# Softmax attention: results copied out of PSUM by ScalarE, the split a step later, one gate projection beside the first softmax

## The reference

```python
# first block, layer 2: 16 heads of 64, 4 kv heads, window 128, context keys, a sink
m = max(max(s_lat), max(s_ctx), sink); p = exp(s - m)
den = sum(p_lat) + sum(p_ctx) + exp(sink - m)
o = (p_lat @ v_lat + p_ctx @ v_ctx) / den;  y = o @ w_out
# second block, each layer: 8 heads of 64, 2 kv heads
q = rope(rms_norm(h @ w_q)); k = rope(rms_norm(h @ w_k)); v = h @ w_v
y_attn = softmax(q k^T / 8) v * silu(h @ w_g)
out = (sigmoid(ga) * (y_attn @ w_br_attn) + sigmoid(gg) * (y_gla @ w_br_gla)
       + sigmoid(gs) * (y_sgu @ w_br_sgu)) @ w_out
```

## Time and profile before

| | |
|---|---|
| median of 3 runs | 3404.61 us (3398.12 to 3415.74) |
| the profiled execution | 3406.66 us, of it a span of 3404.9 us |
| TensorE busy | 3108.3 us (91%) |
| VectorE busy | 1914.2 us (56%) |
| ScalarE busy | 1180.5 us (35%) |
| GpSimd busy | 210.3 us (6%) |
| DMA | 323.92 MB, mean 95 GB/s |
| chain that ended last | TensorE 75%, VectorE 11%, ScalarE 8%, issue 4% |

### The profile page before, as it was taken

The page is one execution under the profiler, slowest core; times in us unless marked ns, Lnnn a source line. Parts: engine busy times, 40 slices in busy tenths (PEclk is TensorE's granted clock), DMA queues, the critical chain, the costliest instruction groups (busy, mean ns, idle before and its releaser), DMA issues.

```text
span 3404.9 us, 43105 instructions
## 1 busy us (share of the span) xinstructions
PE 3108.3 (91%) x17878; PEld 2574.3 (76%) x17878; DVE 1914.2 (56%) x2796; ACT 1180.5 (35%) x1795; POOL 210.3 (6%) x138
## 2 busy tenths in 40 slices
PE   7997889999999788999989899988999998998898
PEld 6877778888886666777877788865788776776677
DVE  7856646656434574777644543457354645455655
ACT  4225342212223454322243333325222543433432
POOL 0003100000010000000000320000000202200000
PEclk9999899999998899999989999999999999999999
DMA  5554123333321002555432222310213222230123
GB/s 209 168 169 137 44 68 125 126 126 126 100 69 60 16 1 64 166 175 175 145 82 70 73 77 73 99 32 1 96 51 129 89 72 84 87 115 26 63 96 124
DMA packets 100091, 323.92 MB, mean 95 GB/s; under 512 B 14310, under 2 KB 20326, under 8 KB 98744
## 3 DMA queue, kind: packets, MB, share of 16 engines
q1 hardware_dynamic: 89812, 291.29, 26.5%
q10 hardware_dynamic: 10084, 29.87, 2.5%
HBM read 301.46 MB, written 19.66 MB: 94 GB/s over the span
## 4 chain that ended last, share of the span: by engine, by line
PE 75%; DVE 11%; ACT 8%; issue 4%; DMA 1%; POOL 1%; ACTq 0%; SPq 0%; DVEq 0%; POOLq 0%
PE PS L388 74%; ACT whi L198 2%; ACT Pq L1289 1%; PE PS L391 1%; DVE STs L1326 1%; ACT nt L622 1%; DVE JUNK L525 1%; DVE stage L525 1%; DVE STq L1326 1%; ACT Ps L1289 1%; DVE wlo L212 1%; DMA Ht<-in_hT 1%; ACT U L627 1%; DVE fg L734 1%; ACT FS L1717 0%
## 5 line engine op out<-in xcount | busy, mean ns | idle before, releaser
L388 PE MATMUL PS<-U,whi 128*128 128x512 f32 (+1 forms) x4992 | 1081.8, 363 | 79.1 <-DVE U L652 27.5
L388 PEld LDWEIGHTS PS<-U,whi 128*128 128x128 f32 x4992 | 839.0, 192 | 253.9 <-issue 42.9
L212 DVE TENSOR_TENSOR wlo<-stage,whi 128x1024 fp32r<-128x1024 f32 x339 | 425.6, 1257 | 995.3 <-ACT whi L198 994.7
L198 ACT ACTIVATE whi<-stage 128x1024 fp32r<-128x1024 f32 x339 | 358.2, 1057 | 1358.8 <-PE PS L388 1329.0
L388 PE MATMUL PS<-Y,whi 128*128 128x512 f32 (+1 forms) x2240 | 581.0, 363 | 22.5 <-DVE Y L736 12.9
L388 PE MATMUL PS<-U,wlo 128*128 128x512 f32 (+1 forms) x2496 | 570.0, 355 | 0.0
L388 PEld LDWEIGHTS PS<-U,wlo 128*128 128x128 f32 x2496 | 421.9, 189 | 73.7
L388 PEld LDWEIGHTS PS<-Y,whi 128*128 128x128 f32 x2240 | 395.5, 190 | 98.4 <-DVE Y L736 14.8
L388 PE MATMUL PS<-Y,wlo 128*128 128x512 f32 (+1 forms) x1120 | 366.8, 362 | 0.0
L388 PE MATMUL PS<-whi,U 128*128 128x512 f32 (+2 forms) x1152 | 326.8, 371 | 16.1 <-DVE mV L1061 6.4
L388 PEld LDWEIGHTS PS<-whi,U 128*128 128x128 f32 x1152 | 208.5, 191 | 59.7 <-issue 11.9
(11 more groups left out here) (432 smaller groups left out, 3116.5 us busy)
## 6 DMA issues: line engine op xcount, KB each, us to landing
stage<-in_w SPq DMA_DIRECT2D x128, 512.0 KB, 4.0
stage<-in_ada SPq DMA_DIRECT2D x80, 512.0 KB, 3.7
stage<-in_adb SPq DMA_DIRECT2D x48, 512.0 KB, 3.7
stage<-in_p_mg SPq DMA_DIRECT2D x16, 512.0 KB, 3.7
stage<-in_p_ma SPq DMA_DIRECT2D x16, 512.0 KB, 3.8
stage<-in_p_ms SPq DMA_DIRECT2D x16, 512.0 KB, 3.8
stage<-in_wo SPq DMA_DIRECT2D x16, 512.0 KB, 3.7
GS<-FS ACTq DMA_DIRECT2D x20, 384.0 KB
```

What stands on the lines that cost most here:

```text
L198: act.activation(self.parts[r % n][0], self.stage[i % len(self.stage)], ACT.Copy).then_inc(*self.S.up("w_hi", i))
L212: dve.tensor_tensor(lo, self.stage[i % len(self.stage)], hi.bitcast(F32), ALU.subtract).then_inc(*self.S.up("w_lo", i))
L388: return pe.matmul(o, l, r, start=start, stop=stop_, skip_group_check=True)
```

## The change

ScalarE copies each tile's `A_OUT` into one of two SBUF buffers `O` (event `a_take`), in the step where `finish` stood; the next values' product waits for that copy. In the grouped attention VectorE then multiplies the buffer by the gate in the same step (`taken`). `finish`, with ScalarE's copy into Y hi and VectorE's subtraction, comes one step later, and the loops have one step more. The last gate tile's projection stands behind the first scores, its sigmoid and product behind the first exponentials and the first scaling (`behind`); the sigmoid writes into the gate's own buffer. In the window attention the six copies of v are shared between VectorE (0 to 2) and ScalarE (3 to 5), the scores no longer wait for v but its product does, and the slot counter is set to 1 ahead of v; in the grouped attention it is set to 2 ahead of gates 1 and 3. Slot 3 is claimed at the first turning, no more ahead of the first scores.

```diff
@@ -1200,13 +1200,16 @@
         class Attention:
-            def __init__(self, tag, offs, ngroups, tiles, query, keys, value, sink=None):
+            def __init__(self, tag, offs, ngroups, tiles, query, keys, value, left, sink=None):
                 self.tag, self.tiles, self.sink = tag, tiles, sink
                 self.query, self.keys, self.value = query, keys, value
+                self.left = left
                 self.P = [place(f"P{tag}{i}", [128, 2, 768], F32, offs + 6144 * i) for i in range(2)]
...
                 self.ST = [place(f"ST{tag}{i}", [128, 4, 2], F32, offs + 18432 + 32 * i) for i in range(3)]
+                self.O = [place(f"O{tag}{i}", [128, 4, 128], F32, offs + 18560 + 2048 * i)[:, :, :] for i in range(2)]
                 self.jobs = [(ti, gi, j) for ti in range(len(tiles)) for gi in range(ngroups) for j in range(4)]
@@ -1219,12 +1222,11 @@
         A_OUT = PS[:, 3584:4096]
-        def pe_attention(pe, a, opened, freed):
+        def pe_attention(pe, a, opened, valued, behind=None):
             N = len(a.jobs)
...
                 pe.wait_ge(*at(*event))
-            B.slot(pe, 3, ("a_o", a.tag))
             for n in range(N + 2):
@@ -1241,12 +1243,17 @@
                     last.then_inc(*up("a_s", a.tag, n))
+                if n == 0 and behind:
+                    behind(pe)
                 if 0 <= n - 2 < N:
...
                     m, c = i // 4, a.width(i)
+                    if i == 0:
+                        for event in valued:
+                            pe.wait_ge(*at(*event))
                     if j == 0 and m:
-                        pe.wait_ge(*at(*freed(m - 1)))
+                        pe.wait_ge(*at("a_take", a.tag, m - 1))
                     pe.wait_ge(*at("a_pta", a.tag, i))
@@ -1265,6 +1272,7 @@
                         B.slot(pe, 2, ("a_t", a.tag))
+                        B.slot(pe, 3, ("a_o", a.tag))
                     for h in range(2):
@@ -1273,12 +1281,15 @@
             B.until[4:6] = [(("a_pta", a.tag, N - 1),)] * 2
-            B.until[6:8] = [(freed(N // 4 - 1), ("a_ptd", a.tag, wide_ones[-1]))] * 2
+            B.until[6:8] = [(("a_take", a.tag, N // 4 - 1), ("a_ptd", a.tag, wide_ones[-1]))] * 2
             B.n = 0
-        def act_attention(act, a, finish):
+        def act_attention(act, a, finish, behind=None):
             N = len(a.jobs)
-            for n in range(N + 2):
+            for n in range(N + 3):
+                if n == 1 and behind:
+                    behind(act)
                 if n < N:
@@ -1299,11 +1310,19 @@
                 if 0 <= n - 2 < N and (n - 2) % 4 == 3:
-                    finish(act, (n - 2) // 4)
-        def dve_attention(dve, a, finish):
+                    m = (n - 2) // 4
+                    act.wait_ge(*at("a_o", a.tag, n - 2))
+                    if m >= 2:
+                        act.wait_ge(*at(*a.left(m - 2)))
+                    act.activation(a.O[m % 2], A_OUT.rearrange("p (f t) -> p f t", t=128), ACT.Copy).then_inc(
+                        *up("a_take", a.tag, m))
+                if 0 <= n - 3 < N and (n - 3) % 4 == 3:
+                    finish(act, (n - 3) // 4)
+        def dve_attention(dve, a, taken, finish, behind=None):
             N = len(a.jobs)
-            for n in range(N + 2):
+            for n in range(N + 3):
                 if 0 <= n - 1 < N:
@@ -1318,6 +1337,8 @@
                         dve.tensor_scalar(p, p, rd[:, h:h + 1], None, ALU.mult).then_inc(*up("a_p", a.tag, i, h))
+                if n == 1 and behind:
+                    behind(dve)
                 if n < N:
@@ -1342,8 +1363,10 @@
                     dve.tensor_copy(a.PT[:, :, 512:c], A_REST[:, :, 0:c - 512]).then_inc(*up("a_ptd", a.tag, i))
-                if 0 <= n - 2 < N and (n - 2) % 4 == 3:
-                    finish(dve, (n - 2) // 4)
+                if 0 <= n - 2 < N and (n - 2) % 4 == 3 and taken:
+                    taken(dve, (n - 2) // 4)
+                if 0 <= n - 3 < N and (n - 3) % 4 == 3:
+                    finish(dve, (n - 3) // 4)
@@ -1379,7 +1402,7 @@
                         lambda gi, h, b: sV[:, b, 128 * gi + 64 * h:128 * gi + 64 * h + 64],
-                        lambda gi, j: sNS[:, 8 * gi + j:8 * gi + j + 5:4])
+                        lambda m: ("s_ylo", m), lambda gi, j: sNS[:, 8 * gi + j:8 * gi + j + 5:4])
         def swa_turned(j):
@@ -1392,8 +1415,10 @@
                     pe_rope(pe, ("s", j - 1), sRM[:, :], swa_turned(j - 1), ("s_qk", j - 1))
-            pe_rows(pe, "sv", [T("sv", u) for u in range(2)], xU, 6, 256, lambda j: (("s_v", 2 * j + 1),))
-            pe_attention(pe, SWA, [("r_done", "s", 9), ("s_v", 5), ("s_mask", 1)], lambda m: ("s_ylo", m))
+            B.n = 1
+            pe_rows(pe, "sv", [T("sv", u) for u in range(2)], xU, 6, 256,
+                    lambda j: (("s_v", min(2 * j + 1, 2)),) if j == 0 else (("s_v", 2), ("s_va", 2 * j + 1)))
+            pe_attention(pe, SWA, [("r_done", "s", 9), ("s_mask", 1)], [("s_v", 2), ("s_va", 5)])
             pe_out(pe, "sout", ("s",), xY, False, [("s_ylo", 7)] * 8)
@@ -1411,11 +1436,13 @@
                 *up("s_mask", 1))
+            for c in range(3, 6):
+                act.activation(sV[:, c, :], rows_of("sv", c, 256), ACT.Copy).then_inc(*up("s_va", c))
             def finish(act, m):
-                act.wait_ge(*at("a_o", "s", 4 * m + 3))
-                act.activation(Y[:, 0, 4 * (m % 2):4 * (m % 2) + 4, 128 * (m // 2):128 * (m // 2) + 128],
-                               A_OUT.rearrange("p (f t) -> p f t", t=128), ACT.Copy).then_inc(*up("s_yhi", m))
+                act.wait_ge(*at("a_take", "s", m))
+                act.activation(Y[:, 0, 4 * (m % 2):4 * (m % 2) + 4, 128 * (m // 2):128 * (m // 2) + 128], SWA.O[m % 2],
+                               ACT.Copy).then_inc(*up("s_yhi", m))
             act_attention(act, SWA, finish)
@@ -1431,16 +1458,17 @@
                 dve_lo(dve, T("sv", u))
+            dve.tensor_scalar(sNS[:, :], col("sink", 0, 16), -1.0, None, ALU.mult).then_inc(*up("s_neg"))
             dve.wait_ge(*at("w_used", T("sv", 1)))
-            for c in range(6):
+            for c in range(3):
                 dve.tensor_copy(sV[:, c, :], rows_of("sv", c, 256)).then_inc(*up("s_v", c))
-            dve.tensor_scalar(sNS[:, :], col("sink", 0, 16), -1.0, None, ALU.mult).then_inc(*up("s_neg"))
+            dve.wait_ge(*at("s_neg"))
             def finish(dve, m):
...
                 dve.wait_ge(*at("s_yhi", m))
-                dve.tensor_tensor(view[1], A_OUT.rearrange("p (f t) -> p f t", t=128), view[0].bitcast(F32),
-                                  ALU.subtract).then_inc(*up("s_ylo", m))
-            dve_attention(dve, SWA, finish)
+                dve.tensor_tensor(view[1], SWA.O[m % 2], view[0].bitcast(F32), ALU.subtract).then_inc(*up("s_ylo", m))
+            dve_attention(dve, SWA, None, finish)
             dve_out(dve, "sout", ("s",), 1, False)
@@ -2077,14 +2105,13 @@
                 self.R = [wide(n + f"r{i}", o1 + 12288 + 2048 * i, 512) for i in range(2)]
-                self.Y = [place(n + f"y{i}", [128, 4, 128], F32, o1 + 18560 + 2048 * i)[:, :, :] for i in range(2)]
                 tiles = [(128 * j, [(0, 768)], []) for j in range(4)]
...
                                       lambda gi, h, k0, m: self.K[64 * h:64 * h + 64, k0:k0 + m],
-                                      lambda gi, h, b: self.V[:, b, 64 * h:64 * h + 64])
+                                      lambda gi, h, b: self.V[:, b, 64 * h:64 * h + 64], lambda m: ("q_ylo", L, m))
             def wide_at(self, j):
@@ -2115,9 +2142,14 @@
                     pe_rope(pe, (L, n - 2), G.RM, G.z(n - 2)[0][:, 0:512], ("q_nz", L, n - 2))
-            for j in range(1, 4):
+            B.n = 2
+            for j in range(1, 3):
                 pe_proj(pe, T(f"p_ag{L}", j), xU, G.full, ("q_g", L, j))
-            pe_attention(pe, G.attn, [("r_done", L, 4), ("q_v", L, 5)], lambda m: ("q_y", L, m))
+            def last_gate(pe):
+                B.n = 2
+                pe_proj(pe, T(f"p_ag{L}", 3), xU, G.full, ("q_g", L, 3))
+            pe_attention(pe, G.attn, [("r_done", L, 4)], [("q_v", L, 5)], last_gate)
             pe_merge(pe, "a", L, G.full, [("q_ylo", L, G.last)] * 4)
@@ -2127,8 +2159,7 @@
                 act.wait_ge(*at("w_used", i))
-                act.wait_ge(*at("q_nz", L, j + 1))
-                act.activation(G.T[(5 + j) % 4][:, 0:G.N], B.of(i)[:, 0:G.N], ACT.Sigmoid).then_inc(*up("q_gs", L, j))
+                act.activation(G.G[:, j, 0:G.N], B.of(i)[:, 0:G.N], ACT.Sigmoid).then_inc(*up("q_gs", L, j))
             for n in range(7):
@@ -2152,25 +2183,27 @@
                         *up("q_rt", L, n - 1))
-            for j in range(1, 4):
+            for j in range(1, 3):
                 gate(j)
-            act.wait_ge(*at("q_g", L, 3))
             def finish(act, m):
...
                 act.wait_ge(*at("q_y", L, m))
```

(29 more changed lines are left out.)

## The result

The changed kernel takes 3419.91 us (median of 12 runs, 3413.58 to 3431.05), the kernel before, on the same chip, 3407.28 (median of 12). The ratio is 1.0034, with a 95% interval of 1.0020 to 1.0048: slower by 12.6 us (medians) or 11.6 (ratio; interval 7 to 16), short of the 0.5% that were to be told from no change. The prediction was 3420.5, from +15.7 us on a median of 3404.61 in 3 runs. That it lies 0.6 us from the result is in part luck: the change added 3 us less than forecast, and the kernel before has a median 2.7 us higher in 12 runs. The profiled execution after took 3419.91 us with a span of 3418.1.

The account below looks back on a forecast made before the run. TensorE is busy 91%, but softmax attention steps are one loop through TensorE, VectorE and ScalarE. Terms 0 + 9.6 + 2.8 + 1.8 + 10.5 - 11.9 - 1.4 + 4.3 = +15.7 us gave 3420.5, range 3400 to 3434.

Parts of the forecast that it names:

- Slots: Projections into four PSUM slots: rows of v wait +1.9, gate 1 +4.7 and +3.9 in the two layers; +10.5 us.
- Grouped finish: Grouped attention: a wide tile pays 1.7 twice where it paid 1.81, +1.6 net; six such tiles, +9.6 us.
- Narrow tiles: First grouped layer's 256-key steps: two more splits at 1.4 us each, +2.8 us.
- Window finish: Window attention, seven finishes: the 1.31 us wait moves one step later and costs the same; sum 0.
- Ends: End of each of three attentions: one more copy in series before the last split, +0.6 us each, +1.8.
- Openings of the grouped attention: Last gate's product to third scores, both layers: gains of 6.9 and 6.2 us, less 0.6 each for clock; -11.9.
- residual of the weight: Grouped opening: a weight's residual (1.26 us) now behind the last gate projection's product, 0.75 of it on the path.
- Opening of the window attention: Ahead of the first window scores: three v copies go to ScalarE, four copies of 0.345 us less wait, -1.4.
- Clock: Clock falls after stalls: 2.0 and 1.8 us at gate 1, 0.5 at v rows, 0 net in loops; +4.3.
- Rival C: Clock falls at nearly every second stall, +1.3 us at 6 tiles and 3 at the openings: 3431; 15%.
- Tables: Gate's sigmoid between exponentials: two more table loads per layer, 1.28 us each, one on the path, no 1380 ns drain.
- VectorE has no slack to hide it: Softmax attention loops: VectorE cannot hide a tile's finish, which costs 1.31 us (window) and 1.81 us (grouped).

Follow-up runs that it names:

- experiment 1: Kernel before with only the slot counter set: 1 ahead of the window stage's rows of v, 2 ahead of each grouped stage's gates; ratio 1.0038.
- experiment 2: Changed kernel with free slots: rows of v from slot 0, gates 1, 2, 3 in slots 3, 2, 3; 3408.78 us, ratio 1.0005 to the kernel before.
- experiment 3: Changed kernel with VectorE's subtraction and its wait for ScalarE's rounded copy one loop step later, ScalarE untouched; ratio 0.9968 to the kernel before.
- experiment 7: Changed kernel with free slots, gate product, ScalarE's rounded copy and VectorE's subtraction each one step behind what it waits for; 3372.42 us, ratio 0.9885 to the kernel before.
- experiment 5: Changed kernel with free slots and VectorE's subtraction one loop step later; 3390.9 us, ratio 0.9947 to the kernel before.
- experiment 6: Changed kernel with free slots, the gate's product and the subtraction moved from VectorE to GpSimd; 3367.24 us, ratio 0.9883 to the kernel before.

## Why the prediction was right, step by step

*Slots: right, and the largest term.* +1.9, +4.7 and +3.9 were predicted, +1.9, +4.6 and +3.8 measured; experiments 1 and 2 put them in and take them out again, both with the clock behind them (13.0, and 10 to 11 for the 11 to 15 expected). Nothing in a trace names a slot; counting the takes did.

*Grouped finish: right in kind, each tile a little less.* Two long periods in a row came as said; +1.32 for a wide tile, not +1.6, since each costs 1.55 and 1.57, not 1.7: 6 x 1.32 = +7.9 for the predicted +9.6. Narrow tiles: periods of 4.09 and 4.10 for 2.62 and 2.61, +3.0 for +2.8.

*Window finish: right.* 7 x (6.45 - 6.41) = +0.3 for 0. Only four of the seven have these periods; the other three stand among narrower steps, with 5.94 and 5.95 for 5.91, 5.91 and 5.79. The loop's other +1.0 lies in single steps in which the clock fell, some 2.4 us after, such as two of 5.85 behind a split (granted clock 0.50 from 1191 to 1193 us for the first), against 1.5 before, in the first steps.

*Ends: right.* TensorE waits 2.18 for 1.51 (window), 2.90 for 2.27 and 2.90 for 2.28: +0.7, +0.6, +0.6. From the last exponential to the next projection it is +1.95, +0.2 and +0.6 all the same: at the window's end the clock fell (mean granted clock 0.51 from 1296 to 1299 us), which takes 1.3 more.

*Openings of the grouped attention: right.* 6.9 and 6.4 gained up to the third scores, 6.9 and 6.2 predicted. For slow third scores I took off 0.6 in each layer; they cost 1.4 in the first and nothing in the second. So -11.9 measured for -11.9. The residual of the weight costs its whole 1.13 behind the product, not 0.75. The third scores come 4.4 us behind the end of the product; I had said 4.

*Opening of the window attention: right.* The first scores wait 3.30 for 4.50, -1.2 for -1.4: four copies less (1.38), while the small negation of the sink, once behind the copies, now stands ahead of them (0.17). With the slots of experiment 2 it is less. There slot 1 holds the third and fourth of the six rows of v, so by the program the scores wait for VectorE's third copy and ScalarE's first; from the last rotation's product to the first scores that kernel takes 20.03, the one before 20.80: -0.8.

*Clock: right in sum.* 1.25 at each gate 1 (2.0 and 1.8 predicted: too much by half) and about 1.5 at the rows of v (0.5 predicted; from their start to the beginning of the wait ahead of the scores 18.79, in experiment 1 17.27): 4.0 for 4.3, an agreement of two errors that cancel. Rival C falls, and with a surprise: in the grouped loops the kernel before lost 2.9 and 1.4 us to such falls, the changed one, the third scores apart, 0.8 and 1.4.

*Tables: the row was right.* Load and sigmoid follow each other without a gap again: 2288.40 + 1.28 = 2289.68, and the sigmoid begins at 2289.69. The drain of some 1380 ns that the Trainium skill ("ScalarE: Activation LUTs", What ACT_TABLE_LOAD costs) adds to each switch isn't in these rows; page and measurement differ, and the measurement decides.

*What failed is a sentence, not the sum.* "VectorE has no slack to hide it": it has, 0.79 us in a bare window step. I read the finish's 1.31 as work in a full chain, and named a wait for ScalarE in the grouped attention only (0.70), though the window's subtraction waits 1.59 in the trace before. Experiments 3 and 7 show that it was the wait for ScalarE, within one step, and that the work itself costs 0 there and 0.41 in a grouped step. As the change left both in the same step, the sum didn't suffer; had it moved VectorE's half by one more step, as experiment 3 does, I would have missed some 20 us.

*Not settled.* Between the stretches, in code that the diff doesn't touch, the shifts move by +2.1, -2.2 and -0.9. They sum to -1.0, and their cause stays open. Added up, the predicted terms measure +14.3 for +15.7: slots 10.3, finishes 0.3 + 7.9 + 3.0, ends 1.9, openings -11.9 and -1.2, clock 4.0. The falls of the clock outside of them (+1.0 in the window loop, +1.3 at its end, -2.1 in the grouped loops), -0.4 at the first grouped end and these -1.0 leave 13.1 of the span's 13.2. Where a fall comes was not predicted by anything here.

## What to carry to other kernels

When a loop goes through several engines and each works in order, put each link of a side chain one step of the loop behind the link that it waits for; a wait inside the step costs the whole loop (1.3 to 1.6 us here), the instruction itself 0 to 0.41. Before judging whether an engine has slack, add up its idle times in a bare step, not in the step with the extra work. And when a projection is moved, count which buffer it and its neighbours now take: here two numbers in the order of four slots cost 13 us, as much as the finish rearranged (12.6) and more than the openings gave (10.9).

## What the runs showed of the hardware

After the same gap of 2.10 us ahead of the rows of v the clock fell in the changed kernel and not in experiment 1: there the granted clock stayed at 1.00 and two matmuls took 0.40, here it went to 0.50 and they took 0.63 for some 3.3 us. So the gap alone doesn't decide a fall.

Removing waits doesn't by itself remove falls: in experiment 5 four of the six long product steps (6.52) are followed by one. Where no long step is left there are none in these traces once the loop runs: not in the window loops of experiments 3, 5, 6 and 7, and not in the steps with 768 keys of experiments 6 and 7, with periods of 4.97 in the one and of 4.97 and 5.38 in the other. That the long steps cause the falls is not shown; the window loop of the kernel before has them at 6.42 and no fall.
